# A modulation chunk of 2048 rows in one VectorE instruction and one 1 MB load, in a fused two-block kernel

## The chip, the cores and the metric

The kernel runs on one core of a Trainium2 chip. The metric is the device time of one execution in microseconds (us), lower is better. TensorE does the matrix products, VectorE (DVE in the profile) and ScalarE (ACT) the elementwise work. The queues of SyncE (SP) and GpSimd (POOL) issue the transfers from memory.

## What is computed

Two blocks in a row on 256 rows of 2048 columns. The first is an adaptive-norm block: all its modulation comes from one vector `c`.

```python
c_act = jax.nn.silu(c)                       # 2048 values
mod = c_act @ w_ada[l] + b_ada[l]            # w_ada: 2048 x 12288
sh1, sc1, gt1, sh2, sc2, gt2 = jnp.split(mod[:, None, :], 6, axis=-1)
h = rmsnorm(x, g_mix[l]) * (1.0 + sc1) + sh1
x = x + gt1 * hybrid_mixer(h, ...)           # pooling, attention, gated recurrence
h = rmsnorm(x, g_ffn[l]) * (1.0 + sc2) + sh2
x = x + gt2 * conv_glu_ffn(h, w_gate, w_up, conv_w, conv_b, w_down)
```

The second block is two more layers of four mixing branches; nothing in them uses `mod`. The change touches only how `mod` is computed: 100 MB of `w_ada`, each number used once.

## The kernel before

**The stream of weight tiles.** All big products run over one stream of 1028 weight tiles, each 128 partitions by 1024 numbers (512 KB), numbered g. SP loads tile g into one of four raw places (`RING = 4`) once VectorE has split tile g-4. ScalarE copies it, rounded, into `w_hi`, VectorE subtracts to get `w_lo` (the "split", L1679 in the front part and L1541 after it), and TensorE does twelve products of 512 columns (L1039 to L1041). ScalarE may write `w_hi` of tile g only when TensorE is done with tile g-4, so at most four split tiles lie ahead of TensorE. Tiles 0 to 135 are the front part (the mixer), from 136 on comes the feed-forward part, then the two layers.

**The modulation.** A block of 128 columns of `w_ada` is one column of `mod`. There are 96 blocks. Each is cut into two chunks of 1024 rows (`PARTS = 2`), so there are 192 chunks of 128 x 1024 numbers, 512 KB each. POOL issues their loads in order (L475). `weigh(i)` (L1606) multiplies a chunk with `c_rows` on VectorE and sums it along the row; the sum of a block's first chunk starts from `b_ada`, that of its second from what the first left in `mod`, and so it waits for the first. Each `weigh` raises `ada_used` by one, and POOL waits for it before it loads into the same place again.

**Places.** Slots are 4 KB a partition. The first 64 chunks (32 blocks) go round nine slots, `ADA_SLOTS = (14, 15, 16, 17, 18, 4, 5, 6, 7)`; the other 128 chunks go round the first five of them (`ADA_RING = 5`), because slots 4 to 7 are then needed for the mixer.

**Order on VectorE.** It is written out by hand. In the front part `upto(t)` does the splits up to tile t, and behind the split of tile g the weighs that `weighs` puts there: the 64 early ones at tiles 2 to 39 (`EARLY_FEEDS`), the next 96 at tiles 44 to 130 (`44 + 87 * late // 96`). The other work of the mixer stands between. The last 32 are in the feed-forward part, one behind each of some 30 splits (`advance(G_FF, ...)`). `residual(n)` (L1669, L1671) adds the mixer's output to `x`.

Of the kernel before, what the change touches and what calls it, by code (L numbers as in the profile page):

```python
# [10 lines left out]
ALU = mybir.AluOpType  # L11
# [11 lines left out]
GT = KD // KC  # L23
# [6 lines left out]
PARTS = 2  # L30
AH = D // PARTS
ADA_RING = 5
ADA_SLOTS = (14, 15, 16, 17, 18, 4, 5, 6, 7)
# [43 lines left out]
CHUNKS = [(n, h) for n in range(len(BLOCKS)) for h in range(PARTS)]  # L77
EARLY = PARTS * M_GATE1
ADA_PLACE = [i % len(ADA_SLOTS) if i < EARLY else (i - EARLY) % ADA_RING for i in range(len(CHUNKS))]
ADA_TURN = [ADA_PLACE[:i + 1].count(p) for i, p in enumerate(ADA_PLACE)]  # L80
ADA_BEFORE = [max((v for v in range(i) if ADA_PLACE[v] == p), default=None) for i, p in enumerate(ADA_PLACE)]
# [100 lines left out]
def build(nc, t):  # L182
    with ExitStack() as ctx:
# [99 lines left out]

        c_rows = slot(12, PARTS, AH)
        ada_at = [slot(i, AH) for i in ADA_SLOTS]

# [77 lines left out]
        ada_in = [sem(f"ada_in{i}") for i in range(len(ADA_SLOTS))]  # L364
# [50 lines left out]
        EARLY_FEEDS = [2 + 38 * i // EARLY for i in range(EARLY)]  # L415
# [619 lines left out]
        def _(pe):  # L1035
# [75 lines left out]
            def broadcast(h, bank):  # L1111

                first = (M_GATE1, M_GATE1 + 8, M_GATE2, M_GATE2 + 8)[h]
                pe.wait_ge(ada_used, PARTS * (first + 8))
# [419 lines left out]
        def _(dve):  # L1534
# [321 lines left out]
            dve.wait_ge(ada_used, PARTS * M_GATE2)  # L1856
# [46 lines left out]
            G2 = PARTS * M_GATE2  # L1903
# [3 lines left out]
            advance(g0, lambda i: weigh(G2 + 2 * GT + i))  # L1907
# [14 lines left out]
            weigh(G2 + 3 * GT + 6)  # L1922
            weigh(G2 + 3 * GT + 7)
# [513 lines left out]
```

## Time and profile before

| | us |
|---|---|
| median of three runs | 3100.82 |
| lowest, highest | 3099.75, 3101.12 |
| the profiled execution | 3100.88 |
| its span, first to last instruction | 3099.1 |
| TensorE busy | 3033.9 |
| VectorE busy | 1999.3 |
| ScalarE busy | 1496.7 |

The profiled execution is 1.8 us longer than its span, and 0.06 us above the median. A share of busy time is a mean over stages that have different limits; so the profile has to be read by stretches of the span. Times on a row count from the start of the span.

### The profile page before, as it was taken

To read this page: it belongs to the slowest core of one execution; us is meant where nothing else is said; L and a number is where in the kernel's file an instruction comes from. 1 tells how busy PE (TensorE), PEld (TensorE's weight loads), DVE (VectorE), ACT (ScalarE), POOL (GpSimd) and SP (SyncE) were. 2 spreads that over 40 slices of the span, in tenths; PEclk is the share of its full clock that TensorE was granted. 3 is DMA by queue.
4 is the path that set the end of the run, shared out by engine and by line. 5 is a ranking of instruction groups with operands and counts; after the bars stand their busy time and mean duration, and the time that the engine had idled before them with its cause. 6 is when DMAs were issued, how large, how long until landed. Compare 5 with 4: busy or idle time off the path is not lost.

```text
span 3099.1 us, 38332 instructions
## 1 busy us (share of the span) xinstructions
PE 3033.9 (98%) x14098; PEld 2523.6 (81%) x14098; DVE 1999.3 (65%) x2277; ACT 1496.7 (48%) x1769; POOL 104.8 (3%) x202
## 2 busy tenths in 40 slices
PE   6899998999999999999999999999999999999999
PEld 5677877888888888888888888888888888888887
DVE  7989888865665666775555565565475655565564
ACT  4555545444544444545444444544545444444543
POOL 2211111100000000000000000000000000000000
PEclk9999999999999999999999999999999999999999
DMA  9988896855556555554556545555455555555555
GB/s 396 387 321 301 315 376 248 341 189 189 184 183 195 187 189 186 166 182 164 193 173 191 177 162 191 169 191 186 167 183 170 192 175 193 171 165 191 170 183 190
DMA packets 179429, 657.11 MB, mean 212 GB/s; under 512 B 19904, under 2 KB 20192, under 8 KB 178528
## 3 DMA queue, kind: packets, MB, share of 16 engines
q1 hardware_dynamic: 151008, 551.28, 52.8%
q0 software_dynamic: 28288, 103.98, 8.9%
q8 instruction: 92, 1.51, 0.2%
q14 instruction: 41, 0.34, 0.0%
HBM read 653.09 MB, written 2.10 MB: 211 GB/s over the span
## 4 chain that ended last, share of the span: by engine, by line
PE 90%; DVE 5%; DMA 2%; issue 1%; ACT 1%; SPq 0%; DVEq 0%; ACTq 0%
PE pg L1039 28%; PE pg L1041 28%; PE pg L1040 28%; DVE R L1606 2%; DMA w_raw<-w 2%; PE pm L1074 1%; DVE w_lo L1679 1%; PE pm L1102 1%; PE pm L1492 1%; DMA R<-w_ada 1%; PE pm L1386 0%; ACT w_hi L579 0%; PE pm L1442 0%; PE pm L1083 0%; PE pm L1116 0%
## 5 line engine op out<-in xcount | busy, mean ns | idle before, releaser
L1541 DVE TENSOR_TENSOR w_lo<-w_raw,w_hi 128x1024 fp32r<-128x1024 f32 x888 | 1085.7, 1225 | 973.7 <-ACT w_hi L500 969.3
L500 ACT ACTIVATE w_hi<-w_raw 128x1024 fp32r<-128x1024 f32 x888 | 940.7, 1060 | 1329.9 <-PE pg L1041 1304.2
L1039 PE MATMUL pg<-w_hi,hT_hi 128*128 128x512 f32 x3200 | 1265.6, 396 | 52.5 <-DVE w_lo L1679 36.5
L1041 PE MATMUL pg<-w_hi,hT_lo 128*128 128x512 f32 x3200 | 1251.4, 391 | 0.0
L1040 PE MATMUL pg<-w_lo,hT_hi 128*128 128x512 f32 x3200 | 1251.0, 391 | 0.0
L1039 PEld LDWEIGHTS pg<-w_hi,hT_hi 128*128 128x128 f32 x3200 | 604.5, 189 | 183.5 <-issue 32.8
L1041 PEld LDWEIGHTS pg<-w_hi,hT_lo 128*128 128x128 f32 x3200 | 604.0, 189 | 127.3
L1040 PEld LDWEIGHTS pg<-w_lo,hT_hi 128*128 128x128 f32 x3200 | 604.8, 189 | 121.7
L1039 PE MATMUL pg<-w_hi,y_parts 128*128 128x512 f32 x864 | 337.6, 391 | 1.4 <-issue 1.4
L1041 PE MATMUL pg<-w_hi,y_parts 128*128 128x512 f32 x864 | 336.3, 389 | 0.0
L1040 PE MATMUL pg<-w_lo,y_parts 128*128 128x512 f32 x864 | 336.1, 389 | 0.0
L579 ACT ACTIVATE w_hi<-w_raw 128x1024 fp32r<-128x1024 f32 x140 | 147.5, 1059 | 174.8 <-PE pg L1041 85.4
L1679 DVE TENSOR_TENSOR w_lo<-w_raw,w_hi 128x1024 fp32r<-128x1024 f32 x140 | 170.4, 1220 | 53.4 <-ACT w_hi L579 52.9
L1039 PEld LDWEIGHTS pg<-w_hi,y_parts 128*128 128x128 f32 x864 | 162.2, 188 | 34.8 <-issue 1.8
L1041 PEld LDWEIGHTS pg<-w_hi,y_parts 128*128 128x128 f32 x864 | 162.2, 188 | 33.8
L1040 PEld LDWEIGHTS pg<-w_lo,y_parts 128*128 128x128 f32 x864 | 162.3, 188 | 33.2
L1606 DVE CUSTOM_DVE_ANT_0 R<-R,mod 128x1024 f32<-128x1024 f32 x96 | 122.8, 1280 | 4.5 <-DMA R<-w_ada 1.7
L1606 DVE CUSTOM_DVE_ANT_0 R<-R,vec_sb 128x1024 f32<-128x1024 f32 x96 | 122.7, 1279 | 0.9 <-DMA R<-w_ada 0.7
L475 POOL DMA_DIRECT2D R<-w_ada x192 | 101.5, 529 | 498.2 <-DVE mod L1606 490.7
L881 ACT ACTIVATE R<-pg,sc 128x512 f32<-128x512 f32 x124 | 77.7, 677 | 0.1
L1074 PEld LDWEIGHTS pm<-con_sb,R 128*128 128x128 f32 x448 | 51.2, 140 | 5.1
L1074 PE MATMUL pm<-con_sb,R 128*128 128x128 f32 x448 | 55.2, 272 | 0.0
(284 smaller groups left out, 1398.5 us busy)
## 6 DMA issues: line engine op xcount, KB each, us to landing
w_raw<-w SPq DMA_DIRECT2D x1028, 512.0 KB, 3.9
R<-w_ada POOLq DMA_DIRECT2D x192, 512.0 KB, 7.4
R<-mem_T SPq DMA_DIRECT2D x4, 512.0 KB, 10.2
x_rows<-x SPq DMA_DIRECT2D x1, 2048.0 KB, 16.2
R<-mem_T SPq DMA_DIRECT2D x1, 2048.0 KB, 12.0
out<-x_rows SPq DMA_DIRECT2D x4, 512.0 KB, 5.0
con_sb<-con SPq DMA_DIRECT2D x1, 1344.0 KB, 16.1
small_w_sb<-small_w POOLq DMA_DIRECT2D x2, 576.0 KB, 5.7
```

What stands on the lines that cost most here:

```text
L475: pool.dma_start(ada_at[ADA_PLACE[i]], t["w_ada"][i]).then_inc(ada_in[ADA_PLACE[i]], 16)
L500: act.activation(w_hi[:, g % RING, :, :].rearrange("p c n -> p (c n)"), raw[:, g % RING, :], ACT.Copy).then_inc(hi_done, 1)
L579: act.activation(w_hi[:, g % RING, :, :].rearrange("p c n -> p (c n)"), raw[:, g % RING, :], ACT.Copy).then_inc(hi_done, 1)
L881: i = act.activation(dest[:, tb, :], src[:, tb, :], func, scale=rs[:, tb:tb + 1])
L1039: pe.matmul(out, hi, w_hi[:, slot, c, :], start=start, stop=False)
L1040: pe.matmul(out, hi, w_lo[:, slot, c, :], start=False, stop=False)
L1041: return pe.matmul(out, lo, w_hi[:, slot, c, :], start=False, stop=stop)
L1074: i = pe.transpose(pm[b][:, c * S + tb * P:c * S + (tb + 1) * P], rows[:, tb, (2 * q + c) * P:(2 * q + c + 1) * P], ident)
L1102: i = pe.matmul(pm[tb][:, h * P:(h + 1) * P], PT[:, h, sb_, tb * P:(tb + 1) * P], v[:, sb_, h * P:(h + 1) * P], start=(sb_ == 0), stop=(sb ...
L1541: tt(flat(w_lo[:, g % RING, :, :]), raw[:, g % RING, :], flat(w_hi[:, g % RING, :, :]).bitcast(F32), ALU.subtract).then_inc(lo_done, 1)
L1606: dve.tensor_tensor_reduce(chunk, chunk, c_rows[:, h, :], 1.0, start, ALU.mult, ALU.add, mod[:, n:n + 1]).then_inc(ada_used, 1)
L1679: tt(flat(w_lo[:, g % RING, :, :]), raw[:, g % RING, :], flat(w_hi[:, g % RING, :, :]).bitcast(F32), ALU.subtract).then_inc(lo_done, 1)
```

## The change

A block of 128 columns by all 2048 rows becomes one chunk. It is one `weigh` instruction (L1632 in the new file) and 8 KB a partition. The wait of a second half for the first goes away, and so does the second start value. In the early part a chunk takes two neighbouring slots of eight: four places, (14,15), (16,17), (4,5), (6,7). Later the chunks go round the five slots 14 to 18 two at a time: (14,15), (16,17), (14,18), (15,16), (17,18), and so on. Where the two slots are neighbours, the load is one transfer of 1 MB. Where they are not (14 and 18), it is two of 512 KB. The weigh of chunk n stands where the first half of it stood, at tile 2 + 38n/32 early and 44 + 87(n-32)/48 later. In the feed-forward part it stands where the second half stood.

```diff
-PARTS = 2
-AH = D // PARTS
-ADA_RING = 5
-ADA_SLOTS = (14, 15, 16, 17, 18, 4, 5, 6, 7)
+AH = D // 2
+ADA_EARLY = (14, 16, 4, 6)
+ADA_LATE = (14, 15, 16, 17, 18)
...
+def ada_slots(n):
+    if n < EARLY:
+        first = ADA_EARLY[n % len(ADA_EARLY)]
+        return (first, first + 1)
+    r = 2 * (n - EARLY)
+    return tuple(sorted(ADA_LATE[(r + h) % len(ADA_LATE)] for h in range(2)))
+
+def ada_loads(n):
+    a, b = ada_slots(n)
+    return [(a, 0, D)] if b == a + 1 else [(a, 0, AH), (b, AH, D)]
+
+def ada_before(n):
+    return max((m for m in range(n) if set(ada_slots(m)) & set(ada_slots(n))), default=None)
...
-            for i in range(len(CHUNKS)):
-                if ADA_BEFORE[i] is not None:
-                    pool.wait_ge(ada_used, ADA_BEFORE[i] + 1)
-                pool.dma_start(ada_at[ADA_PLACE[i]], t["w_ada"][i]).then_inc(ada_in[ADA_PLACE[i]], 16)
-                if i == EARLY + 11:
+            for n in range(len(BLOCKS)):
+                if ada_before(n) is not None:
+                    pool.wait_ge(ada_used, ada_before(n) + 1)
+                for at, first, last in ada_loads(n):
+                    pool.dma_start(slot(at, last - first), t["w_ada"][n][:, first:last]).then_inc(ada_in[at], 16)
+                if n == EARLY + 5:
...
-                n, h = CHUNKS[i]
-                chunk = ada_at[ADA_PLACE[i]]
-                dve.wait_ge(ada_in[ADA_PLACE[i]], 16 * ADA_TURN[i])
-                start = V("b_ada")[:, n:n + 1]
-                if h:
-                    dve.wait_ge(ada_used, i)
-                    start = mod[:, n:n + 1]
-                dve.tensor_tensor_reduce(chunk, chunk, c_rows[:, h, :], 1.0, start, ALU.mult, ALU.add,
+                chunk = ada_at(n)
+                for at, _, _ in ada_loads(n):
+                    dve.wait_ge(ada_in[at], 16 * ada_turn(at, n))
+                dve.tensor_tensor_reduce(chunk, chunk, c_rows, 1.0, V("b_ada")[:, n:n + 1], ALU.mult, ALU.add,
                                          mod[:, n:n + 1]).then_inc(ada_used, 1)
...
-            advance(G_FF, lambda i: weigh(G2 + i))
-            advance(G_FF + 1, lambda i: weigh(G2 + GT + i))
+            def weigh_gate(first, i):
+                if i % 2:
+                    weigh(M_GATE2 + first + i // 2)
+            advance(G_FF, lambda i: weigh_gate(0, i))
+            advance(G_FF + 1, lambda i: weigh_gate(4, i))
```

VectorE at the start, from the split of tile 2 on, before (R is the chunk, `ISA` is the weigh and the small instruction behind it that writes its sum):

```order
L1679 TENSOR_TENSOR w_lo<-w_raw,w_hi 128x1024 [waits hi_done]
L1606 ISA R,mod<-R,vec_sb 128x1024 [waits ada_in0,c_ready]
L1606 ISA mod 128x1
L1606 ISA R,mod<-R,mod 128x1024 [waits ada_used,ada_in1]
L1606 ISA mod 128x1
L1710 TENSOR_TENSOR hT_lo<-R,hT_hi 128x1024 [waits hT_hi_done]
L1679 TENSOR_TENSOR w_lo<-w_raw,w_hi 128x1024 [waits hi_done]
L1606 ISA R,mod<-R,vec_sb 128x1024 [waits ada_in2]
```

The same place after the change:

```order
L1704 TENSOR_TENSOR w_lo<-w_raw,w_hi 128x1024 [waits hi_done]
L1632 ISA R,mod<-R,vec_sb 128x2048 [waits ada_in14,c_ready]
L1632 ISA mod 128x1
L1735 TENSOR_TENSOR hT_lo<-R,hT_hi 128x1024 [waits hT_hi_done]
L1704 TENSOR_TENSOR w_lo<-w_raw,w_hi 128x1024 [waits hi_done]
L1632 ISA R,mod<-R,vec_sb 128x2048 [waits ada_in16]
```

Two weighs with a wait on `ada_used` between them have become one of twice the length.

VectorE near the end of the front part, tiles 128 to 131, before:

```order
L1679 TENSOR_TENSOR w_lo<-w_raw,w_hi 128x1024 [waits hi_done]
L1606 ISA R,mod<-R,vec_sb 128x1024 [waits ada_in4]
L1606 ISA mod 128x1
L1644 TENSOR_TENSOR hT_lo<-R,hT_hi 128x512 [waits hT_hi_done]
L1679 TENSOR_TENSOR w_lo<-w_raw,w_hi 128x1024 [waits hi_done]
L1606 ISA R,mod<-R,mod 128x1024 [waits ada_used,ada_in0]
L1606 ISA mod 128x1
L1644 TENSOR_TENSOR hT_lo<-R,hT_hi 128x512 [waits hT_hi_done]
L1858 TENSOR_TENSOR mod<-mod,vec_sb 128x8x2 [waits ada_used]
L1679 TENSOR_TENSOR w_lo<-w_raw,w_hi 128x1024 [waits hi_done]
L1669 TENSOR_TENSOR R<-pg,R 128x1024 [waits bc_done,tile_used]
```

And after, from the split of tile 129 on (tile 128 has no weigh now):

```order
L1704 TENSOR_TENSOR w_lo<-w_raw,w_hi 128x1024 [waits hi_done]
L1632 ISA R,mod<-R,vec_sb 128x2x1024 [waits ada_in18,ada_in14]
L1632 ISA mod 128x1
L1669 TENSOR_TENSOR hT_lo<-R,hT_hi 128x512 [waits hT_hi_done]
L1704 TENSOR_TENSOR w_lo<-w_raw,w_hi 128x1024 [waits hi_done]
L1669 TENSOR_TENSOR hT_lo<-R,hT_hi 128x512 [waits hT_hi_done]
L1883 TENSOR_TENSOR mod<-mod,vec_sb 128x8x2 [waits ada_used]
L1704 TENSOR_TENSOR w_lo<-w_raw,w_hi 128x1024 [waits hi_done]
L1694 TENSOR_TENSOR R<-pg,R 128x1024 [waits bc_done,tile_used]
```

One weigh behind every tile has become a double one behind about every second tile, and the last stands a tile earlier. The chunk in slots 14 and 18 waits for both its loads.

POOL's queue from its first load on, before (`x67` counts equal rows; `band` is a load of the mixer):

```order
L475 DMA R<-w_ada 128x1024 [waits mem_in0]
L475 DMA R<-w_ada 128x1024 x8
L475 DMA R<-w_ada 128x1024 [waits ada_used] x67
L478 DMA R<-band 128x2048 [waits zf_ps]
L475 DMA R<-w_ada 128x1024 [waits ada_used] x116
```

And after:

```order
L505 DMA R<-w_ada 128x2048 [waits mem_in0]
L505 DMA R<-w_ada 128x2048 x3
L505 DMA R<-w_ada 128x2048 [waits ada_used] x30
L505 DMA R<-w_ada 128x1024 [waits ada_used]
L505 DMA R<-w_ada 128x1024
L505 DMA R<-w_ada 128x2048 [waits ada_used] x3
L508 DMA R<-band 128x2048 [waits zf_ps]
```

Four loads of 1 MB go out at once where there were nine of 512 KB; `band` stands behind 38 whole chunks where it stood behind 76 halves.

## Rows read from the trace of the kernel before

**Rows 1.** The page, busy time, share of the span and instructions of each engine.
```profile
PE 3033.9 (98%) x14098; PEld 2523.6 (81%) x14098; DVE 1999.3 (65%) x2277; ACT 1496.7 (48%) x1769; POOL 104.8 (3%) x202
```
**Rows 2.** Whom TensorE waited for in the whole span: us, times, longest.
```profile
PE pg L1039 <- DVE w_lo L1679: 36.5, 13, 13.2
PE pg L1039 <- ACT R L584: 7.9, 1, 7.9
```
**Rows 3.** Stretches: us, busy PE, PEld, DVE, ACT, POOL; PE clock, DMA share, GB/s.
```profile
0.00:57.00 57.00, 36.21 (x132) 27.37 (x132) 38.40 (x54) 28.37 (x28) 12.94 (x28) 0.97 0.99 391
57.00:81.00 24.00, 20.10 (x108) 17.66 (x109) 21.47 (x42) 12.25 (x26) 4.53 (x9) 0.86 1.03 409
81.00:105.70 24.70, 23.90 (x109) 19.34 (x108) 24.21 (x37) 16.13 (x24) 6.54 (x13) 1.00 1.00 385
105.70:142.00 36.30, 26.88 (x108) 21.40 (x108) 35.13 (x51) 17.50 (x26) 7.93 (x15) 0.91 1.02 401
142.00:168.00 26.00, 22.36 (x97) 16.86 (x96) 25.68 (x37) 11.62 (x14) 2.11 (x4) 1.00 0.72 259
...
300.00:422.00 122.00, 121.44 (x609) 102.60 (x608) 103.13 (x141) 53.94 (x78) 21.12 (x40) 1.00 0.91 337
422.00:482.00 60.00, 55.05 (x232) 45.26 (x233) 57.26 (x72) 28.00 (x39) 10.02 (x19) 0.94 0.96 363
...
630.00:3099.00 2469.00, 2460.64 (x11476) 2052.91 (x11474) 1455.56 (x1541) 1177.75 (x1342) 1.59 (x3) 1.00 0.55 181
```
**Rows 4.** DVE in order of time, 21 to 22 us and 149 to 159 us: start, length, instruction.
```profile
21.60 1.28 DVE L1606 CUSTOM_DVE_ANT_0 R<-R,vec_sb 128x1024 f32<-128x1024 f32 x1
...
149.07 1.27 DVE L1606 CUSTOM_DVE_ANT_0 R<-R,vec_sb 128x1024 f32<-128x1024 f32 x1
...
150.50 1.29 DVE L1606 CUSTOM_DVE_ANT_0 R<-R,mod 128x1024 f32<-128x1024 f32 x1
...
157.02 1.28 DVE L1606 CUSTOM_DVE_ANT_0 R<-R,vec_sb 128x1024 f32<-128x1024 f32 x1
...
158.22 1.22 DVE L1679 TENSOR_TENSOR w_lo<-w_raw,w_hi 128x1024 fp32r<-128x1024 f32 x1
```
**Rows 5.** Groups of DVE instructions with shapes kept apart: busy us, mean ns, idle before.
```profile
L1606 DVE CUSTOM_DVE_ANT_0 R<-R,vec_sb 128x1024 f32<-128x1024 f32 x96 | 122.7, 1279 | 0.9 <-DMA R<-w_ada 0.7
...
L1580 DVE TENSOR_TENSOR R<-R,sc 128x1024 f32<-128x1024 f32 x8 | 9.8, 1226 | 0.3
...
L1580 DVE TENSOR_TENSOR R<-R,sc 128x2048 f32<-128x2048 f32 x2 | 4.6, 2292 | 0.1
```
**Rows 6.** DMA queues, 14 to 24 us: packets, MB, share of 16 engines.
```profile
q0 software_dynamic: 567, 2.06, 51.7%
q1 hardware_dynamic: 566, 2.06, 51.2%
```
**Rows 7.** The same, 24 to 38 us (`x`, 2 MB, goes through q1 then).
```profile
q1 hardware_dynamic: 585, 3.71, 64.0%
q0 software_dynamic: 583, 2.13, 38.1%
```
**Rows 8.** Chain that ended last, 100 to 170 and 404 to 430 us: start, us, what.
```profile
105.71 13.39 DMA w_raw<-w
...
135.42 4.91 DMA w_raw<-w
...
406.67 16.75 DMA w_raw<-w
```
**Rows 9.** Loads of chunks, 425 to 482 and 520 to 560 us: KB, median us to landing.
```profile
R<-w_ada POOLq DMA_DIRECT2D x19, 512.0 KB, 5.3
...
R<-w_ada POOLq DMA_DIRECT2D x16, 512.0 KB, 8.6
```
**Rows 10.** DVE in order of time, 415 to 490 us, with the idle time before.
```profile
424.54 1.23 DVE L1679 TENSOR_TENSOR w_lo<-w_raw,w_hi 128x1024 fp32r<-128x1024 f32 x1 [5.78 <-ACT w_hi L579]
...
489.01 1.22 DVE L1679 TENSOR_TENSOR w_lo<-w_raw,w_hi 128x1024 fp32r<-128x1024 f32 x1
```

More of the change, by code:

```diff
@@ L76, with ada_turn @@
 BLOCKS += [5 * KD + k for k in range(KD)]
[L77 to L81, printed above, removed]
+EARLY = M_GATE1
+def ada_slots(n):
[7 more added lines that the diff above has]
+    return [(a, 0, D)] if b == a + 1 else [(a, 0, AH), (b, AH, D)]
+def ada_turn(slot, n):
+    return sum(load[0] == slot for m in range(n + 1) for load in ada_loads(m))
+def ada_before(n):
+    return max((m for m in range(n) if set(ada_slots(m)) & set(ada_slots(n))), default=None)
 IN2 = 15
@@ L282, in build, with ada_at @@
         sq_1 = hf_1.rearrange("p k s -> p (k s)").rearrange("p (a d) -> p a d", a=TB)
-        c_rows = slot(12, PARTS, AH)
-        ada_at = [slot(i, AH) for i in ADA_SLOTS]
+        c_rows = slot(12, 2, AH)
+        def ada_at(n):
+            a, b = ada_slots(n)
+            if b == a + 1:
+                return slot(a, 2, AH)
+            return slot(a, b - a + 1, AH)[:, 0:b - a + 1:b - a, :]
         Zx, Zy, Zp = slot(0, TB, NW), slot(2, TB, NW), slot(8, TB, NW)
@@ L363, in build @@
         mem_in = [sem(f"mem_in{i}") for i in range(4)]
-        ada_in = [sem(f"ada_in{i}") for i in range(len(ADA_SLOTS))]
+        ada_in = {i: sem(f"ada_in{i}") for i in sorted(set(ADA_EARLY + ADA_LATE))}
         raw_in = [sem(f"raw_in{i}") for i in range(RING)]
@@ L414, in build @@
         FRONT_SSQ = TB + TB * NB
-        EARLY_FEEDS = [2 + 38 * i // EARLY for i in range(EARLY)]
+        WEIGH_FEEDS = [2 + 38 * n // EARLY for n in range(EARLY)]
+        WEIGH_FEEDS += [44 + 87 * n // (M_GATE2 - EARLY) for n in range(M_GATE2 - EARLY)]
         def front_bank(u, tb=slice(None)):
@@ L1113, in broadcast @@
                 first = (M_GATE1, M_GATE1 + 8, M_GATE2, M_GATE2 + 8)[h]
-                pe.wait_ge(ada_used, PARTS * (first + 8))
+                pe.wait_ge(ada_used, first + 8)
                 for m in range(8):
@@ L1634, in _ @@
             weighs = {}
-            for i in range(PARTS * M_GATE2):
-                late = i - EARLY
-                weighs.setdefault(EARLY_FEEDS[i] if late < 0 else 44 + 87 * late // 96, []).append(i)
+            for n, feed in enumerate(WEIGH_FEEDS):
+                weighs.setdefault(feed, []).append(n)
             outs_at = {F_END[F_OUT + n] - 1 + RING: n for n in range(NB)}
@@ L1901, in down_out @@
                 tt(F_, F_, pg[n % 2][:, :, :], ALU.add).then_inc(evac_dve, 1)
-            G2 = PARTS * M_GATE2
-            advance(G_FF, lambda i: weigh(G2 + i))
-            advance(G_FF + 1, lambda i: weigh(G2 + GT + i))
+            def weigh_gate(first, i):
[3 more added lines that the diff above has]
+            advance(G_FF + 1, lambda i: weigh_gate(4, i))
             g0 = G_FF + 2
-            advance(g0, lambda i: weigh(G2 + 2 * GT + i))
+            advance(g0, lambda i: weigh_gate(8, i))
             conv(0)
@@ L1913, in _ @@
                 split(g0 + 2, (i,))
-                weigh(G2 + 3 * GT + i)
+                if i % 2:
+                    weigh(M_GATE2 + 12 + i // 2)
             down_out(g0 + 2, 0, 0)
@@ L1921, in _ @@
             down_out(g0 + 2, 0, 3)
-            weigh(G2 + 3 * GT + 6)
-            weigh(G2 + 3 * GT + 7)
+            weigh(M_GATE2 + 15)
             with dve.Fori(1, NFF - 2) as j:
@@ L2377 @@
     w_ada = a["w_ada"][0]
-    ada = [w_ada[h * AH:(h + 1) * AH, BLOCKS[n] * P:(BLOCKS[n] + 1) * P].T for n, h in CHUNKS]
+    ada = [w_ada[:, n * P:(n + 1) * P].T for n in BLOCKS]
     def ff(name, j):
```

6 lines of the change are left out of this document (3 added, 3 removed).

## The prediction

> **What bounds the kernel now.** Read the page's first section first: TensorE is busy 98% of the span, so only its idle time and its slow stretches are to be won [rows 1]. Then see whom it waited for: 36.5 us in 13 waits for the split of a tile by VectorE, 7.9 us once for a ScalarE copy [rows 2]. Then see where, in the table of stretches [rows 3]. From 630 us to the end TensorE is busy 2460.6 of 2469 us, and no chunk is weighed there; nothing in that part can change. From 300 to 422 us it is busy 121.4 of 122, though VectorE weighs there too. The loss lies in 0 to 168 us and in 422 to 520 us.
>
> In 0 to 168 us two resources are near their limits at once. The DMA engines carry 385 to 409 GB/s at a share of 0.99 to 1.03 up to 142 us, and only from 142 to 168 us do they fall to 259 GB/s. VectorE is busy 21.5 of 24, 24.2 of 24.7, 35.1 of 36.3 and 25.7 of 26 us in the four stretches behind 57 us [rows 3]. So a shorter weigh helps only where VectorE is last. Where the tile itself is late, it does not.
>
> **The instruction.** A weigh takes 1.28 us and is pipelined: one that starts at 157.02 has the next instruction start at 158.22, so it costs 1.20 us. Where the second half follows directly, it starts 1.43 us behind the first (149.07 to 150.50), because it waits for the first's result [rows 4]. The trace has no weigh of 2048 numbers. The nearest rows are the tensor products of L1580: 1226 ns for 1024, 2292 for 2048, so 1.07 us for 1024 more [rows 5]. A whole chunk should cost 1.20 + 1.07 = 2.27 us. The two halves cost 2.40 apart and 2.63 in a row. The gain is 0.13 or 0.36 us a chunk. The placement formulas put both halves at one tile in 14 of the 32 early blocks and in 6 of the 48 later ones. Bounds: no gain but the wait (0.23 us in 20 of 80 blocks, 4.6 us of VectorE's time), and the full 20 x 0.36 + 60 x 0.13 = 15 us. I take the full one, since L1580 is nearly the same work. Most of it falls where VectorE isn't last.
>
> **Start, to 57 us: +2.0.** The first weigh starts at 21.60 us [rows 4], behind the split of tile 2. Both queues are full by then, and how they share matters. From 14 to 24 us q0 (chunks) and q1 (tiles) move 567 and 566 packets and the same 2.06 MB. At 412 GB/s (4.12 MB in 10 us, rows 6) a 0.52 MB tile lands every 3.8 us instead of every 2.5 while chunks are queued. The first four chunks are 4.2 MB; at 275 GB/s they occupy their queue for 15 us, in which SP's queue gets 2.1 MB instead of 3.1. Its pieces (a quarter of the memory rows, a tile, and so on) reach tile 2 some 5 us later. After that the ring is full, SP has the engines alone, and tile 6 lands about when it did. VectorE has 2.6 to 3 us less work up to its row norm behind tile 10 (8 chunks), and it was busy only 38.4 of the 57 us [rows 3]. So the norm comes later by 5 - 3 = 2 us. Bounds: -1 (the waits swallow it) and +5.
>
> The Trainium skill, page "DMA: Bandwidth & Descriptors", section "Queues, rings and completion order", says that each DMA engine goes round the queues that have work and changes at packet borders. The two stretches agree, packet for packet. It speaks against this change: fair sharing by packets (+2.0) stands against +0.0 or less with sharing by bytes.
>
> **57 to 119 us: -1.5.** TensorE's transposes and ScalarE set 57 to 81 us. From 81 to 105.7 us VectorE is last (24.2 of 24.7 us busy, rows 3). Six chunks stand there, three of them with both halves in a row: 3 x 0.36 + 3 x 0.13 = 1.5 us. Then tile 27, loaded at 105.71, takes 13.39 us to land [rows 8], behind 1.1 MB of other loads of SP. TensorE waits 7.9 us for the ScalarE copy that stands behind it [rows 2]. That is DMA rate. Chunks are asked for at VectorE's pace, so as many bytes compete as before; the chunk ring holds half a megabyte less, but what it holds goes first. I take 0, bounds -2 and +2. Larger packets may carry more: 5.84 MB in 14 us is 417 GB/s against 412 [rows 6, 7], 1% of the 82 us that 33.5 MB of chunks take, -1 at best; I take 0.
>
> **119 to 168 us: -0.8.** One direct pair before 134 us gives -0.4. Tile 34 (135.42, 4.91 us to landing, rows 8) is on the chain: eight of its packets an engine meet chunk packets of double length, up to +1.2; I take +0.8. From 141 to 166 us VectorE is busy all the time (25.7 of 26 us from 142 on) and six chunks take 13.6 instead of 14.9 us: -1.3. Sum: -0.9, rounded to -0.8. Together, TensorE's steady stretch behind 168 us starts at +2.0 - 1.5 - 0.8 = -0.3.
>
> **168 to 422 us: -0.7.** TensorE is the bound but for 250 to 300 us, where five chunks lie on VectorE's path: 5 x 0.13. A double weigh also holds up one attention head by 1.1 us and relieves the next; I take nothing for it, bounds -0.5 and +1. Else the new ring of two and a half must only keep up. Chunk n+2 may be loaded when chunk n is weighed, and is wanted two periods less one weigh later. A period is 1.8 tiles, 122/35 x 1.8 = 6.3 us here (35 tiles), so 10 us are there for a load. A 512 KB load takes 5.3 to 8.6 us to land, and that with others of its own queue ahead of it [rows 9].
>
> **422 to 520 us: -1.0.** Tile 113 is loaded at 406.67 and lands 16.75 us later [rows 8]; VectorE waits 5.78 us for it, till 424.54 [rows 10]. The second half of that block now falls into this wait. From there to 482 us VectorE is busy 57.3 of 60 us [rows 3] and 19 halves (22.8 us) become 9 chunks (20.4 us): -2.4. But at tile 120 the split can come only some 1.2 us earlier, since ScalarE waits for TensorE. I count -1.9. A period is 4.5 to 5.1 us here, which leaves 6.8 to 8 us for a load, and 5.7 where two chunks stand at tiles 120 and 121. A 1 MB load should take 5.3 + 1.3 us (eight more packets an engine): +0.9 once. The split of tile 132 at 489.01, behind `residual` and the second norm, moves by the sum, and TensorE with it.
>
> **520 us on: 0.** TensorE needs 5.4 us for two tiles, and one chunk and two tiles are 2.1 MB, 5.1 us at 412 GB/s. It has the room, but little. Bound: +3.
>
> The sum: -0.3 - 0.7 - 1.0 + 0 = -2.0 us. From the profiled execution, 3100.88 - 2.0 = **3098.9 us** (the median of before is 3100.82, so it makes no difference which is taken).
>
> The same page's section "Bandwidth" advises loads of 1 MiB or more for three quarters of the peak rate. Here queued 512 KB loads already give 412 GB/s [rows 6], so I count nothing for it.
>
> **Rivals.**
> *All of VectorE's saving arrives.* If tiles do not come later at the start and the DMA engines are not the limit, 0 to 168 us gain 14 x 0.36 + 18 x 0.13 = 7.4 us, and the later stretches 0.7 + 2.4: 3090.4 us. For it: VectorE's busy share behind 57 us. Against it: the DMA share of 1.0 and the packet counts.
> *The ring of two is too short: slower.* In 520 to 560 us a 512 KB load takes 8.6 us to land [rows 9]. If a chunk of 1 MB takes 9.9, a chunk can be weighed only every (9.9 + 2.3)/2 = 6.1 us, against 5.1 us in 425 to 482 and 5.4 in the feed-forward part. That costs 9 x 1.0, less some 4 us of split tiles in hand, and 16 x 0.7, less the same: 5 + 7 = +12, so 3111 us. It decides from a landing time of 8.6 us on. Against it: those 8.6 us held two or three loads of the same queue, and now there is one.
> *Tiles starve at the start: slower.* The 5 us of the first weigh are not won back, and tile 27 lands 2 us later: +5 + 2 - 1.5 - 0.8 - 0.7 - 1.0 = +3, 3103.9 us.
> *The change of length brings nothing* (a 2048 weigh costs two of 1024): the waits alone, about 3100.
>
> **How the numbers follow.** Forecast, with some us to each side: 0.45. All the saving: 0.22. Short ring: 0.13. Starved start: 0.15. No gain by length: 0.05. The range runs from 3091, near the second case, to 3108, between starved start and short ring; about 2 in 10 lie outside. A measurement of this kernel tells about 0.2%, 6.2 us, from no change. Faster than 3094.6 takes nearly all of the saving case and a little of the forecast: 0.25. Slower than 3107.0: the short ring and a part of the starved start: 0.17. The rest is within: 0.58.
>
> **What would show it.** The weigh near 2.35 us long, 96 times. The first one near 26 us instead of 21.6, and the norm behind tile 10 about 2 us later. Packets of 8 KB in q0, and q1 with a third of the bytes up to 24 us. Waits of the weigh for its load of under 5 us in all. TensorE's first product of tile 140 about 2 us earlier than before, and from there to the end the same time. The forecast is wrong if weighs wait for their loads by more than 10 us in all, or if TensorE is idle behind 520 us.

## The result, and the profile after

The changed kernel takes **3116.11 us** (median of 5 runs, 3114.09 to 3123.57), against 3100.82 us before (5 runs, 3099.00 to 3101.12). The ratio is 1.0056, with a 95% interval of 1.0042 to 1.0071: slower by 15 us, where 3098.9 and at most 3108 were forecast. The profiled execution took 3120.26 us, its span is 3118.5 us, so its trace is 19.4 us longer than that of before and 4 us above the median.

First the page: TensorE's work is the same, VectorE's is smaller (1999.3 in [rows 1]), and q0 carries its 104 MB in 16,336 packets. The weighs themselves are as long as forecast:

```profile
PE 3035.4 (97%) x14098; PEld 2523.6 (81%) x14098; DVE 1984.8 (64%) x2085; ACT 1496.0 (48%) x1769; POOL 60.9 (2%) x119
...
q0 software_dynamic: 16336, 103.98, 9.0%
...
L1632 DVE CUSTOM_DVE_ANT_0 R<-R,vec_sb 128x2048 f32<-128x2048 f32 x96 | 225.4, 2347 | 30.8 <-DMA R<-w_ada 30.7
```

The end of the last row is the first bad sign: VectorE stands idle for 30.7 us ahead of weighs, until the chunk has landed. It was 0.9 us for the first halves before [rows 5], and 2.4 us for all chunks, in three waits. The waits of TensorE and VectorE (us in all, times, longest), TensorE's over the whole span, VectorE's from 0 to 660 us:

```profile
PE pg L1069 <- DVE w_lo L1704: 38.8, 20, 13.2
PE pg L1069 <- ACT R L614: 16.4, 1, 16.4
...
PE pg L1069 <- DVE w_lo L1571: 5.0, 3, 2.5
...
DVE R L1632 <- DMA R<-w_ada: 30.7, 18, 4.8
```

The single wait of 7.9 us for ScalarE [rows 2] has become one of 16.4. The stretches of [rows 3] again, with 482 to 630 us added (columns as there):

```profile
0.00:57.00 57.00, 35.25 (x125) 25.88 (x126) 35.95 (x38) 25.55 (x26) 6.12 (x15) 0.97 0.98 397
57.00:81.00 24.00, 19.55 (x112) 16.91 (x111) 21.57 (x33) 13.47 (x27) 2.11 (x4) 0.93 0.96 366
81.00:105.70 24.70, 24.70 (x115) 20.55 (x114) 23.78 (x27) 14.18 (x20) 3.69 (x7) 1.00 0.93 358
105.70:142.00 36.30, 17.81 (x64) 13.74 (x63) 23.78 (x26) 14.34 (x21) 3.17 (x6) 0.72 0.88 345
142.00:168.00 26.00, 24.54 (x111) 19.79 (x110) 25.86 (x26) 13.53 (x20) 2.64 (x5) 1.00 0.88 338
300.00:422.00 122.00, 120.50 (x609) 101.94 (x608) 103.18 (x109) 59.88 (x91) 12.63 (x24) 1.00 0.89 324
422.00:482.00 60.00, 49.12 (x207) 39.34 (x205) 46.65 (x43) 22.76 (x32) 5.78 (x11) 0.94 0.89 342
482.00:630.00 148.00, 135.49 (x602) 110.26 (x602) 119.12 (x119) 74.77 (x94) 11.05 (x21) 0.98 0.79 289
```

Two places stand out. From 105.7 to 142 us TensorE is busy 17.8 us instead of 26.9, and from 422 to 482 us 49.1 instead of 55.1 while VectorE falls from 57.3 to 46.7. VectorE was busy nearly all the time in both before (35.1 of 36.3 and 57.3 of 60 us); now it waits itself, 23.8 us busy in the first and 46.7 in the second.

Where the 19.4 us arise is plainest from TensorE's first product of each tile. This table is worked out from the traces: the start of a tile in a kernel less its start in the kernel before, in us. The last column is the landing of tile 27 behind its issue.

| kernel | 2 | 25 | 39 | 111 | 124 | 140 | 168 | 208 | tile 27 |
|---|---|---|---|---|---|---|---|---|---|
| before, start | 21.8 | 121.1 | 167.3 | 418.6 | 462.2 | 520.1 | 599.7 | 712.0 | 13.4 |
| the changed kernel | +4.1 | +10.6 | +9.8 | +9.2 | +14.2 | +15.9 | +17.4 | +19.3 | 24.3 |
| e1_half_loads | +1.5 | -1.3 | -1.9 | +1.6 | +6.7 | +8.2 | +14.4 | +19.8 | 14.3 |
| e2_two_weighs | +4.5 | +4.4 | +4.4 | +6.6 | +12.5 | +15.6 | +21.8 | +24.0 | 16.4 |
| e3_half_rings | +0.2 | 0.0 | -0.4 | +0.3 | +2.1 | +3.1 | +1.5 | +2.8 | 14.1 |
| e4_short_ring | +1.1 | -0.9 | -0.9 | +0.9 | +4.4 | +6.1 | +7.1 | +10.1 | 13.5 |
| e5_local_halves | +4.1 | +1.6 | +0.6 | +0.1 | +3.4 | +4.0 | +5.2 | +7.6 | 14.8 |
| e6_late_halves | +5.0 | +6.5 | +6.4 | +5.9 | +7.6 | +7.2 | +5.6 | +7.0 | 20.0 |
| e7_moved | +4.8 | -2.4 | +1.4 | +3.6 | +7.3 | +8.6 | +7.8 | +8.8 | 11.6 |
| e9_before_moved | +0.5 | -7.3 | -2.2 | -2.2 | -2.0 | -0.4 | -2.0 | -2.1 | 7.4 |
| e10_single_early | +0.2 | -1.5 | -1.9 | -1.3 | -1.4 | -1.4 | -1.3 | -1.4 | 13.7 |
| e11_single_moved | +0.2 | -8.0 | -5.1 | -4.8 | -4.7 | -4.6 | -4.6 | -4.6 | 7.7 |
| e8_rings_moved | +0.6 | -9.9 | -6.8 | -5.6 | -3.8 | -2.7 | -4.3 | -3.1 | 7.6 |

The table shows one execution of each kernel; the runs of one kernel spread over 2 to 10 us, so a single row tells sizes only roughly. At tile 24 the changed kernel is level (+0.6). Tile 25 loses 10 us at one stroke. It holds to tile 111, and from tile 112 to tile 176 another 10 us go in small steps. Behind that, nothing changes.

**The front.** The chain that ended last, 100 to 170 us (start, us, what), against [rows 8]; then the DMA queues of the changed kernel (packets, MB, share of 16 engines), 14 to 24 us, as in [rows 6], and 95 to 116 us:

```profile
105.36 24.34 DMA w_raw<-w
```
```profile
q0 software_dynamic: 379, 2.83, 67.9%
q1 hardware_dynamic: 378, 1.36, 33.9%
```
```profile
q0 software_dynamic: 764, 5.52, 62.9%
q1 hardware_dynamic: 923, 3.24, 38.2%
```

Tile 27 is issued at the same time as before and lands 24.3 us later instead of 13.4. At the start both queues (q0 carries the chunks, q1 the tiles) move the same number of packets, and the tiles' queue a third of the bytes, 136 KB a us instead of 206. From 95 to 116 us it moves 154 KB a us; in the kernel before, 95 to 110 us, it moved 2.56 MB, 171 KB a us.

**The late part.** First VectorE in order of time (start, length, instruction, idle time before it), then POOL, which issues the chunk loads, in the same stretch:

```profile
426.99 2.35 DVE L1632 CUSTOM_DVE_ANT_0 R<-R,vec_sb 128x2048 f32<-128x2048 f32 x1 [4.77 <-DMA R<-w_ada]
...
547.28 2.35 DVE L1632 CUSTOM_DVE_ANT_0 R<-R,vec_sb 128x2048 f32<-128x2048 f32 x1 [1.22 <-DMA R<-w_ada]
...
552.96 2.35 DVE L1632 CUSTOM_DVE_ANT_0 R<-R,vec_sb 128x2048 f32<-128x2048 f32 x1 [0.61 <-DMA R<-w_ada]
...
561.08 2.35 DVE L1632 CUSTOM_DVE_ANT_0 R<-R,vec_sb 128x2048 f32<-128x2048 f32 x1 [3.49 <-DMA R<-w_ada]
```
```profile
544.08 0.53 POOL L505 DMA_DIRECT2D R<-w_ada  x1 [4.02 <-DVE mod L1632]
549.93 1.04 POOL L505 DMA_DIRECT2D R<-w_ada  x2 [5.33 <-DVE mod L1632]
555.61 0.53 POOL L505 DMA_DIRECT2D R<-w_ada  x1 [4.63 <-DVE mod L1632]
```

The chain that ended last runs through the same place (start, us, what):

```profile
550.45 10.50 DMA R<-w_ada
561.08 2.35 DVE R L1632
```

It is a closed loop: a load is issued as soon as a weigh ends (547.28 + 2.35, so 549.93), lands up to 10.5 us later, and the weigh that waits for it starts then (561.08). The landing medians of chunk loads, 425 to 482 us and 520 to 560 us, against [rows 9]:

```profile
R<-w_ada POOLq DMA_DIRECT2D x7, 1024.0 KB, 8.2
...
R<-w_ada POOLq DMA_DIRECT2D x3, 1024.0 KB, 8.8
```

### The profile page after: what moved, and what is told of

Same layout as the page of the kernel before. It is cut to its first block, busy times and chain, and to the rows that moved or that the text cites. A ratio compares the mean times of both kernels' runs of the same rounds, so it can differ in the third digit from the quotient of the medians.

```text
span 3118.5 us, 37976 instructions
## 1 busy us (share of the span) xinstructions
PE 3035.4 (97%) x14098; PEld 2523.6 (81%) x14098; DVE 1984.8 (64%) x2085; ACT 1496.0 (48%) x1769; POOL 60.9 (2%) x119
## 3 DMA queue, kind: packets, MB, share of 16 engines
q0 software_dynamic: 16336, 103.98, 9.0%
## 4 chain that ended last, share of the span: by engine, by line
PE 87%; DVE 7%; DMA 4%; ACT 1%; issue 1%; SPq 0%; POOL 0%; ACTq 0%; DVEq 0%
PE pg L1069 27%; PE pg L1071 27%; PE pg L1070 27%; DVE R L1632 3%; DMA w_raw<-w 3%; DMA R<-w_ada 2%; DVE w_lo L1704 2%; PE pm L1104 1%; PE pm L1132 1%; PE pm L1522 1%; DVE w_lo L1571 1%; PE pm L1416 0%; ACT w_hi L609 0%; PE pm L1472 0%; PE pm L1113 0%
## 5 line engine op out<-in xcount | busy, mean ns | idle before, releaser
L1070 PEld LDWEIGHTS pg<-w_lo,hT_hi 128*128 128x128 f32 x3200 | 604.9, 189 | 121.1
L1632 DVE CUSTOM_DVE_ANT_0 R<-R,vec_sb 128x2048 f32<-128x2048 f32 x96 | 225.4, 2347 | 30.8 <-DMA R<-w_ada 30.7
L505 POOL DMA_DIRECT2D R<-w_ada x109 | 57.5, 529 | 563.9 <-DVE mod L1632 558.5
L1926 DVE TENSOR_TENSOR R<-R,pg 128x1024 f32<-128x1024 f32 x44 | 53.4, 1215 | 0.0
## 6 DMA issues: line engine op xcount, KB each, us to landing
R<-mem_T SPq DMA_DIRECT2D x1, 2048.0 KB, 13.5
```

The lines of the kernel that those rows point to most:

```text
L505: pool.dma_start(slot(at, last - first), t["w_ada"][n][:, first:last]).then_inc(ada_in[at], 16)
L1070: pe.matmul(out, hi, w_lo[:, slot, c, :], start=False, stop=False)
L1632: dve.tensor_tensor_reduce(chunk, chunk, c_rows, 1.0, V("b_ada")[:, n:n + 1], ALU.mult, ALU.add, mod[:, n:n + 1]).then_inc(ada_used, 1)
L1926: tt(F_, F_, pg[n % 2][:, :, :], ALU.add).then_inc(evac_dve, 1)
```

## The experiments

Three theories could explain the loss. **P**: packets of 8 KB leave the tiles' queue too little. **R**: the ring is too short, since a load waits for the weigh of two chunks before. **L**: one long instruction holds up the splits. The times of a group of runs stand beside a median of before from the same chip (3100.43 us for the first four, 3100.23 for the next four, 3101.01 for the last three). Where two runs' medians are subtracted below and one is the changed kernel's, its own before had 3100.82, so up to 0.6 us of such a difference may be the chip's.

### Packets alone

```
-    return [(a, 0, D)] if b == a + 1 else [(a, 0, AH), (b, AH, D)]
+    return [(a, 0, AH), (b, AH, D)]
```

 Then tile 27 lands about 13 to 15 us after its issue again instead of 24.3, TensorE's 16.35 us wait before tile 25 falls back to about 8, and the time is 3104 to 3107 us, some 10 us under the changed kernel; waits of the weigh for its load behind 420 us stay. Rival R (the ring is too short, whatever the packets): the time stays at 3113 to 3117. Rival L (a weigh of 2.35 us holds up the splits): also 3113 to 3117.

Measured: 3118.92 us, ratio 1.0061 (1.0044 to 1.0077). In front P was right: tile 27 lands after 14.3 us and tile 39 is at -1.9. That front had four places for whole chunks too, so the shorter ring isn't what costs there. But the end is no better, 2.8 us above the changed kernel and above every range that was given. From tile 111 to 208 this kernel loses 18.2 us where the changed one loses 10.1. VectorE waits 54.2 us for chunks, 30 times. A possible reason: late the chunk is what VectorE waits for, 8 KB packets give its queue more than the half that it gets with 4 KB, and a single weigh needs both halves. That is argued, not shown, and the next two runs show that it doesn't hold for every weigh.

### Two weighs instead of one

`weigh(i)` is called for each half again, at the feeds of the kernel before; loads, slots and POOL's wait stay those of the changed kernel:
```
+                n, h = i // 2, i % 2
+                chunk = ada_at(n)[:, h, :]
...
-                    pool.wait_ge(ada_used, ada_before(n) + 1)
+                    pool.wait_ge(ada_used, 2 * (ada_before(n) + 1))
```

> The changed kernel with its 1 MB loads and its ring, but two weighs of 1024 numbers for each chunk, at the places that they had before the change. Theory P: the instruction has no part in the loss, tile 27 still lands 22 to 25 us after its issue, and the time is 3114 to 3119 us (the shorter instruction path is lost). Rival L: the long instruction was the cause, and the time falls to 3101 to 3105.

Measured: 3123.83 us, ratio 1.0075 (1.0058 to 1.0091). The loss doesn't go away with the long instruction: without it the kernel is 7.7 us slower still, above the range that P gave. VectorE waits 54.2 us, 29 times. P missed in front too: tile 27 lands after 16.4 us, not 22 to 25, and tile 25 is at +4.4. The extra loss is late: 17.4 us from tile 111 to 208 against 10.1. It can't be read as the price of the instruction alone, since the edit also keeps a place taken longer: a place is free only behind the second half's weigh, which stands up to a tile later, and the first half's weigh must wait for the whole 1 MB load.

The short ring with before's loads, which is the edit of the first run on top of this one:

> Two weighs of 1024 numbers and loads of 512 KB as before the change, but the places and the waits of the changed kernel: four places for whole chunks early, two and a half later, and a chunk's place is free only when all of it is weighed. So against the kernel before, only the ring changes. Rival R alone for the whole loss: 3112 to 3117 us. Theory P: the ring explains only the part behind 420 us, 3103 to 3107 us.

Measured: 3111.94 us, ratio 1.0040 (1.0026 to 1.0055), 5 us over P's range and at the lower edge of R's. Tile 39 stands at -0.9, the end at +10.1, and weighs wait 39.1 us in 27 places. Packet size and instruction are those of before, and the number of slots is the same late (eight instead of nine early); what differs in the late part is POOL's wait. So R alone costs 10 us in the trace and 11.5 by the medians, all of it behind tile 39. POOL in order of time shows it, in this kernel and then in the kernel before:

```profile
546.07 1.05 POOL L505 DMA_DIRECT2D R<-w_ada  x2 [5.80 <-DVE mod L1637]
550.97 1.10 POOL L505 DMA_DIRECT2D R<-w_ada  x2 [3.85 <-DVE mod L1637]
```
```profile
549.25 0.53 POOL L475 DMA_DIRECT2D R<-w_ada  x1 [3.13 <-DVE mod L1606]
551.75 0.53 POOL L475 DMA_DIRECT2D R<-w_ada  x1 [1.97 <-DVE mod L1606]
554.32 0.53 POOL L475 DMA_DIRECT2D R<-w_ada  x1 [2.04 <-DVE mod L1606]
```

Before, a half is loaded after every weighed half. In the new ring both halves of a chunk wait until the chunk two before is done, though the slot of one of them came free a chunk earlier. Five slots then do the work of four.

Four kernels share the places and POOL's wait, and differ in packets and weighs alone (with two weighs a place is free only behind the second; the chunks in slots 14 and 18 come by 512 KB loads in all four):

| | 8 KB packets (1 MB loads) | 4 KB packets (512 KB loads) |
|---|---|---|
| single weigh, median | 3116.11 (the changed kernel) | 3118.92 (e1_half_loads) |
| two weighs, median | 3123.83 (e2_two_weighs) | 3111.94 (e4_short_ring) |
| single weigh, lost from tile 111 to 208 | 10.1 | 18.2 |
| two weighs, lost from tile 111 to 208 | 17.4 | 9.2 |

In the short ring neither edit has a sign of its own. Small packets cost 2.8 us with a single weigh and win 11.9 with two; the single weigh wins 7.7 with big loads and costs 7.0 with small ones. So L isn't ruled out for the short ring with small loads, and why the two edits act together like this is open.

### Own slots

```
-                if ada_before(n) is not None:
-                    pool.wait_ge(ada_used, ada_before(n) + 1)
                 for at, first, last in ada_loads(n):
+                    if ada_before(at, n) is not None:
+                        pool.wait_ge(ada_used, ada_before(at, n) + 1)
```
with 512 KB loads in a round of nine slots for the early blocks and five for the late ones.

> One weigh of 2048 numbers a chunk, as in the changed kernel, but the loads as before the change: halves of 512 KB round nine slots early and five later, and each half's load waits for its own slot alone, not for both. Theory P with R: neither loss is left, the gain of the single weigh remains, and the time is 3092 to 3099 us, under the kernel before (3100.8). Rival L: the long instruction costs, and the time is 3104 or more.

Measured: 3102.41 us (10 runs), ratio 1.0006 (0.9997 to 1.0016), between P+R's 3099 and L's 3104. The single weigh stays, and nearly all of the loss is gone: the loads and the ring together account for 13.7 of the 15.3 us. Waits for chunks fall to 18.9 us. What is left in the trace, 2.5 us between tiles 111 and 208, goes with the single weigh, which takes both halves at one moment and frees both at one moment. Most of it comes at one place: at 422.8 us a weigh waits 6.15 us for its chunk, and tile 112 is 2.1 us later against before than tile 110.

### Front and late part apart

```
-    return [(a, 0, D)] if b == a + 1 else [(a, 0, AH), (b, AH, D)]
+    return [(a, 0, D)] if b == a + 1 and not 18 <= n < 27 else [(a, 0, AH), (b, AH, D)]
```

> The changed kernel with one edit: chunks 18 to 26, whose loads stand in their queue between 95 and 135 us, come as two loads of 512 KB with 4 KB packets; all others stay 1 MB loads. Theory P-local (the 10.6 us that TensorE loses at tile 25 are the share of the engines that 8 KB packets take from the tiles' queue while chunk loads are queued, in this window alone): tile 27 lands 14 to 16 us behind its issue instead of 24.3, TensorE's first product of tile 25 is 0 to +2 us against the kernel before instead of +10.6, and behind 422 us the late ring loses what it loses in the changed kernel (+9 to +11 us): the end at 3108 to 3112 us. Rival (the loss in front is one of the whole stretch, not of this window): tile 25 stays at +6 or more, the end at 3115 us.

Measured: 3109.55 us, ratio 1.0032 (1.0019 to 1.0045). Nine chunks with small packets take away the loss at tile 25 (+1.6 instead of +10.6, landing 14.8 us), though tile 2 is still 4.1 us late. P-local holds. Where chunk packets of 4 KB stand beside it, tile 27 lands 13.4 to 14.8 us behind its issue in six traces, and where they are 8 KB 16.4 to 24.3 us in three (the kernels with the small loads where they were).

The other half of the change, undone behind the 32nd block only:

> The early part (blocks up to the 32nd, to about 168 us) exactly as in the changed kernel: 1 MB loads, four places. The late part: each half of a chunk is a 512 KB load that waits for its own slot of five alone, the 2048-number instruction stays. Theory (the two losses are separate: P in front, R behind 422 us): TensorE's tile 25 at +10 to +11 us, tile 111 at +9 us, the end at +11 to +13 us: 3111 to 3114 us, weigh's waits for its loads near 19 us. Rival (a delay of the front is given back later when the late ring keeps up, since a later start leaves TensorE and the loads at the same distance): the end at 3103 to 3107 us.

Measured: 3110.76 us, ratio 1.0037 (1.0023 to 1.0051), just under its range. The late part adds 1.1 us from tile 111 on and nothing is given back, as the theory said. VectorE's waits for chunks are 10.3 us, fewer than the 19 expected. But the front lost 6.5 us at tile 25 here, not the 10 to 11 expected, with code and loads that are the same as in the changed kernel up to there. So the front's loss differs from one execution to the next. By the medians, the local edit is worth 6.6 us and the late one 5.4, and the loads and the ring undone in both places (e3) 13.7. By the traces the two are worth more, 11.7 and 12.3 us at the end, because the traced execution of the changed kernel was 4 us above its median and that of e6_late_halves 2.8 below. So the sum is firm, and its split between front and late part only to some us.

### The small loads ahead of tile 27

```
-                if g == 26:
+                if g == 28:
                     sp.dma_start(b_f, t["b_f"]).then_inc(fw_in, 16)
                     sp.dma_start(small_w[:, 0:KD * 8 + 8 * P], t["front_w"]).then_inc(fw_in, 16)
+                if g == 40:
                     sp.dma_start(con1, t["con1"]).then_inc(cons1_in, 16)
                     sp.dma_start(pool_w, t["pool_w"]).then_inc(cons1_in, 16)
```
In the changed kernel:

> The changed kernel with the 1.1 MB of small loads that stand ahead of tile 27 in the tiles' queue moved: the 576 KB of front_w (and b_f) behind the wait of tile 28, the 512 KB of con1 and pool_w behind that of tile 40. Same bytes, same chunks. Theory P (the tiles' queue gets about a third of the engines, 137 KB a us, so 1.1 MB ahead of tile 27 cost 8 us): tile 27 lands 14 to 17 us behind its issue instead of 24.3, tile 25 at +1 to +4 us instead of +10.6, and the end at 3107 to 3111 us. Rival (the bytes between 95 and 130 us are what counts, wherever they stand): the wait moves to the tiles 28 to 32 and tile 39 stays at +8 or more, the end at 3114 to 3117 us.

Measured: 3113.93 us (4 runs, 3108.04 to 3118.16), ratio 1.0048 (1.0031 to 1.0065). In the trace the theory holds: tile 25 at -2.4, tile 39 at +1.4, the end at +8.8, and tile 27 lands after 11.6 us, even sooner than said. The median is 3 us over the range. The two low runs agree with the trace and the two high ones don't, and those have no trace; which place they lose at is open.

In the kernel before:

> The kernel before with the same small loads moved (front_w to tile 28, con1 and pool_w to tile 40). TensorE's 7.9 us of idle time at tile 25 is then the same queue's doing: at half of the engines' 412 KB a us the 1.1 MB cost 5.3 us. Theory: tile 27 lands 8 to 9 us behind its issue instead of 13.4, the idle time at tile 25 is 2 to 4 us, tile 39 at -2 to -5 us, and the end at 3096 to 3099 us. Rival (what is moved only makes other tiles late, since the engines are full up to 142 us): the end at 3100 to 3102 us.

Measured: 3099.24 us (10 runs), ratio 0.9997 (0.9988 to 1.0007): no difference that can be told. The trace says why. Tile 27 lands after 7.4 us, TensorE's idle time at tile 25 falls from 7.9 to 2.0 us, and 7.3 us are won there. Five tiles on it waits again, 4.1 us at tile 30, for a split that stands behind VectorE's row norm. Of 7.3 us, 2.2 are left in the trace, and by the medians 1.0. VectorE was the next in line.

### Single weighs where they cost nothing

> The kernel before with one edit: the 32 early blocks are weighed by one instruction of 2048 numbers each, at the place of their first half; the loads stay 512 KB in a round of nine, and from the 33rd block on everything is as before. Theory (with 4 KB packets and each half in its own slot nothing is lost in front, and VectorE's saving there falls where a tile is late anyway): TensorE's tile 39 at -1 to +1 us against the kernel before, nothing lost behind 168 us, the end at 3099 to 3102 us, and weigh's waits for loads of 5 to 7 us, all before 168 us. Rival (VectorE's saving arrives in front once the late ring takes nothing back): tile 39 at -3 us or earlier, the end at 3096 to 3098 us.

Measured: 3099.58 us (11 runs), ratio 0.9997 (0.9988 to 1.0006). Single weighs in front win 1.4 us in the trace (tile 39 at -1.9) and lose nothing late, where VectorE waits 0.2 us for a chunk. The edit of `weigh` for both runs of this part, with `V("b_ada")` as the start and `ada_used` raised by two (`whole(i)` weighs both halves; it stands at the tile of the first half, and the two places of a pair are put in the order of their slots):
```
+                if i < EARLY:
+                    if h:
+                        whole(i)
+                    return
```
With the small loads moved as well:

> The kernel before with single weighs for the 32 early blocks, as in the run beside it, and with the 1.1 MB of small loads moved from ahead of tile 27 to tiles 28 (front_w) and 40 (con1, pool_w). With the loads moved alone TensorE was 7.3 us earlier at tile 25 but only 2.2 at tile 34, since it then waited 4.1 us for a split behind VectorE's row norm. Theory (behind the moved loads VectorE is last in 105 to 145 us, so its saving counts there: one pair in a row and two or three others are 0.8 to 1.2 us before that norm): the wait at tile 30 falls to about 3 us, tile 39 at -3 to -4 us, the end at 3096 to 3098 us. Rival (a weigh that needs both halves at once waits for the loads instead): tile 39 at -1 to -2 us, the end at 3098 to 3101 us.

Measured: **3097.22 us** (11 runs, 3095.12 to 3098.22), ratio 0.9988 (0.9979 to 0.9997), faster than both kernels; its slowest run is below the fastest of the 27 runs of before beside it (3098.49). The wait at tile 30 is 2.2 us instead of 4.1, tile 39 is at -5.1. TensorE from 105.7 to 142 us (columns of [rows 3]):

```profile
105.70:142.00 36.30, 29.79 (x113) 22.71 (x111) 36.20 (x38) 18.26 (x26) 8.97 (x18) 0.91 1.03 410
```
It is busy 2.9 us more than before, and VectorE is now busy for the whole stretch. Each edit alone gave 1.4 us or less by the median (1.4 and 1.0), both 3.8. That fits the theory that VectorE's savings arrive once the tile is there in time. The 1.4 us by which both are more than the sum are within the noise of three such differences, though, so the waits at tile 30 (4.1 and 2.2 us) carry the argument, not the medians.

> The changed kernel's single weighs everywhere, 512 KB loads that each wait for their own slot (nine early, five late), and the small loads moved to tiles 28 and 40. Against the run with single weighs for the early blocks only it differs in the late part alone: chunks behind the 32nd are weighed whole, not by halves. Theory (the late loss of a single weigh is that it takes both halves at one time and frees both at one time): 2 to 3 us later at the end than the run with single weighs early, tile 111 the same, its weighs waiting some 12 us for loads behind 422 us: 3098 to 3101 us. Rival (the late waits fall into slack when the front is earlier): the same time within 1 us.

Measured: 3099.23 us (11 runs), ratio 0.9996 (0.9987 to 1.0005), 2.0 us above the run with single weighs in front only. Its trace is even 0.8 us ahead at tile 111 and loses 2.5 us behind it, as e3 did. So the size of the late single weigh's loss comes out a second time. Its mechanism doesn't as it was expected: behind 422 us the weighs wait 2.2 us for chunks, not some 12. The long wait comes before that:

```profile
415.95 2.35 DVE L1634 CUSTOM_DVE_ANT_0 R<-R,vec_sb 128x2048 f32<-128x2048 f32 x1 [5.17 <-DMA R<-w_ada]
```

In e11_single_moved the weigh of a half waits 1.3 us at this place (413.3 us). Why the whole chunk is there 2.7 us later than a half of one is open.

## Why the prediction was wrong, point by point

**The instruction: right.** 2.35 us long, 96 times, and 2.26 us from its start to the next instruction's; forecast 2.35 and 2.27. VectorE has 14.5 us less work. That never was the question.

**Start, to 57 us: right in kind and nearly in size.** The first weigh starts at 25.71 us (forecast near 26), q1 has a third of the bytes, and TensorE's tile 11 is 2.4 us late (forecast +2.0). The tile that counts for VectorE's norm was late as worked out, and the rival with a starved start was not what happened at this place.

**57 to 119 us: the first failed term.** It was -1.5, with "I take 0, bounds -2 and +2" for tile 27. Between tiles 11 and 25 it was +8.2 in this trace and +4.8 in that of e6_late_halves. The reason given was that chunks are asked for at VectorE's pace, so as many bytes compete as before. They were not: chunks 18 to 25 landed 3.8 us apart from 102.7 to 129.5 us, 8 to 12 us behind their issue, so the chunks' queue had work all the time, and where both queues have work the packets decide, as I had worked out for the start. The same arithmetic stood in the paragraph on the start and was not applied here. Between tile 26's landing and tile 27's, 1.1 MB of small loads and a tile pass, 1.62 MB by the sum of the queue's packets. That took 9.2 us before (109.91 to 119.10); at a third of 412 KB a us it is 11.8, and the tiles ahead were already late by the same rule. Counted on the packets of q1, as many bytes were through at 124.3 us as before at 119.1: 5.2 us of rate. The other 5.4 us aren't explained by the rate (last section).

**119 to 168 us:** forecast -0.8, and from tile 25 to tile 39 it was -0.8. From 142 us on VectorE is busy all the time again (25.86 of 26 us), and there its shorter work counts. None of the three parts of the forecast (-0.4, +0.8, -1.3, which add up to -0.9) was measured by itself, so that the sums agree may be luck.

**168 to 422 us:** forecast -0.7, measured -0.6 (tiles 39 to 111). The 10 us that I gave a load were enough for TensorE. They weren't always enough for VectorE, which waited 8.4 us for chunks before 422 us, five times, in room that TensorE had to spare.

**422 to 520 us: the second failed term, -1.0 forecast, +6.7 measured** (tiles 111 to 140). The room (6.8 to 8 us) was worked out rightly from the period. The load was not: I took 6.6 us, from a median of 5.3 us for loads of half the size and 1.3 us more, while the measured 1 MB loads take 8.2 us. That 5.3 was no property of the load's size: loads of 512 KB in the same stretch take 6.6 us in e4_short_ring, 7.1 in e6_late_halves, 7.5 in e1_half_loads and 7.7 in e3_half_rings. So the landing time taken was too short for 512 KB loads of another kernel already, and 1.3 us more didn't make it one for 1 MB. What failed with it is the overlap: with loads this late, VectorE waits for the chunk and TensorE for VectorE (five waits for chunks, 11.8 us in all, from 422 to 520 us). The rival had named the limit right ("from a landing time of 8.6 us on"), and its chance was cut to 0.13 by one argument, that 8.6 us held two or three loads of one queue. A 1 MB load is two such loads.

**520 us on: the third, 0 with a bound of +3; measured +3.4.** The 1 MB loads take 8.8 us from 520 to 560 us. Waits of 0.6 to 3.5 us come at eight chunks from 547 us on. The room that I saw (5.1 of 5.4 us) was one of rate, but in a ring of two the weigh of chunk n+2 can't come sooner than the weigh of chunk n and a landing behind it (8.8 + 2.3 us for two periods of 5.4).

In sum: up to tile 39 the trace shows +9.8 (some 6 by the medians of e5_local_halves and the changed kernel) where -0.3 stood, and from there on +9.5 where -1.7 stood. Both of the forecast's own signs of failure were met: 30.7 us of waits against 10, and TensorE idle behind 520 us (5.0 us for splits against 2.5 before, and 1.6 us for another VectorE result). The short-ring rival, 3111 us, was the nearest to the truth, with the right mechanism; its size, +12, is near the +10.1 measured, but as +5 and +7 in the two stretches where +6.7 and +3.4 came, and it lacked the front. The range ended at 3108 because it took in one slower case at a time, and here two came together.

## What to carry to other kernels

Count the places of a ring by what a load waits for, not by bytes: a ring of two and a half chunks in which a chunk waits as a whole is a ring of two, and it cost 10 us here. Where two queues have work for long, packet size sets their shares: here 8 KB beside 4 KB packets took the tiles' queue from 206 to 136 KB a us at the start (14 to 24 us), and in front they cost some 6 us in all. Don't count on the other side of it: over the whole kernel the larger loads won 2.8 us with one weigh and cost 11.9 with two. And look behind a wait before you price its removal: 7.3 us won at tile 25 were 2.2 us nine tiles later, since VectorE was the next in line.

## What the hardware did that I had not expected

With unequal packets a load lands later than its queue's bytes explain. The trace's packet records tell when the 128 packets of `front_w` (4608 bytes each) started: over 4.4 us in the kernel before (107.4 to 111.8), over 9.0 us in the changed kernel (109.8 to 118.8), 8.5 in e2_two_weighs, 6.6 in e6_late_halves and 4.3 in e5_local_halves, where the chunk packets of that moment are 4 KB again. The kernel takes a tile as landed when all 16 increments of its load's semaphore have come, so its slowest part counts. Its landing can be set against the moment at which as many bytes of the queue had passed as in the kernel before (worked out from the packet records, us):

| kernel | chunk packets | bytes through | tile 27 landed | behind |
|---|---|---|---|---|
| before | 4 KB | 119.1 | 119.1 | 0.0 |
| the changed kernel | 8 KB | 124.3 | 129.7 | 5.4 |
| e6_late_halves | 8 KB | 124.0 | 125.6 | 1.6 |
| e2_two_weighs | 8 KB | 121.7 | 123.5 | 1.8 |
| e5_local_halves | 4 KB | 120.5 | 120.7 | 0.3 |
| e1_half_loads | 4 KB | 118.0 | 117.8 | -0.2 |

Nor do the times of the runs tell: the changed kernel's 5 runs spread over 9.5 us and e7_moved's 4 over 10.1, but e2_two_weighs' 4, with 8 KB packets too, over 3.7, and e8_rings_moved's 11, with 4 KB, over 6.3. What sets a part of a load back is open.

A second point is the packet's own price. In [rows 6] 567 packets of mostly 4 KB took 51.7% of 16 engines for 10 us, 146 ns each; here 379 packets of mostly 8 KB took 67.9%, 287 ns each. Twice the size is twice the time, and the engines carry nearly the same, 412 and 419 KB a us, so larger packets had 2% to win. The Trainium skill, page "DMA: Bandwidth & Descriptors", section "Bandwidth", advises loads of 1 MiB or more. Here the gain in rate from them was those 2%; where they replaced loads of half the size in the same ring, the kernel became 11.9 us slower with two weighs (e4 to e2) and 2.8 us faster with one (e1 to the changed kernel).
